# Four dense units, index items, stream loads and key turns moved forward in two stages of a streaming encoder

## What is computed

```python
s = einsum('bqhd,bld->bqhl', qi, ki) * (IDX_DIM ** -0.5)      # 8 index heads of 64
score = einsum('bqhl,bqh->bql', relu(s), w)                   # masked by chunks of 64 frames
_, idx = lax.top_k(score, topk)                               # 256 of up to 1024; streams: 132 of 528
logits = einsum('bqhgd,bqjhd->bqhgj', q, k_sel) * (A_HEAD_DIM ** -0.5)
p = softmax(where(valid, logits, -inf))
o = einsum('bqhgj,bqjhd->bqhgd', p, v_sel)                    # 16 heads, 4 key/value heads, of 64
```

## Time and profile before

| | us |
|---|---|
| median of 3 runs | 3180.77 (3178.53 to 3181.86) |
| the profiled execution | 3184.14 |
| its span, first to last instruction | 3182.3 |
| proj0b, SP's first issue to its last round's end | 104.2 to 347.7 |
| attention, first issue to last output | 349.0 to 759.9 |

### The profile page before, as it was taken

How to read it: one execution, slowest core, us unless ns; L and a number is a source line. 1 busy time by engine, 2 the same in 40 slices (tenths; PEclk the granted TensorE clock), 3 DMA queues, 4 the chain that set the end, 5 groups by cost and what they waited for, 6 DMA issues and landing times. The chain is left out here.

```text
span 3182.3 us, 45684 instructions
## 1 busy us (share of the span) xinstructions
PE 2982.0 (94%) x17935; PEld 2769.5 (87%) x17935; DVE 1612.6 (51%) x2629; ACT 927.6 (29%) x1640; POOL 699.6 (22%) x404
## 2 busy tenths in 40 slices
PE   8799489997999999999998999988899999999999
PEld 8699478887989999899997989987799999899897
DVE  3499689994253444444434145544334443444435
ACT  3332255664132112121123044433132112121122
POOL 2111010110212111121112145545222111211112
PEclk9899799998999999999999999998999999999999
DMA  4421521123211110111102233327321110110101
GB/s 139 97 73 56 139 60 28 33 49 134 77 63 40 40 53 26 53 40 40 53 27 105 69 111 103 100 84 273 122 68 49 39 53 26 53 48 31 53 28 72
DMA packets 196202, 222.96 MB, mean 70 GB/s; under 512 B 27793, under 2 KB 172113, under 8 KB 196066
## 3 DMA queue, kind: packets, MB, share of 16 engines
q1 hardware_dynamic: 155666, 157.13, 16.1%
q10 hardware_dynamic: 40400, 63.97, 6.1%
HBM read 171.11 MB, written 49.95 MB: 69 GB/s over the span
## 5 line engine op out<-in xcount | busy, mean ns | idle before, releaser
L769 DVE TENSOR_TENSOR h<-mlp_dn_acc,h 128x512 f32<-128x512 f32 x576 | 397.5, 691 | 339.5 <-PE mlp_dn_acc L739 339.5
L758 DVE TENSOR_TENSOR mlp_sq<-mlp_relu 128x384 f32<-128x384 f32 x192 | 165.9, 864 | 555.8 <-ACT mlp_relu L662 555.8
L724 PE MATMUL mlp_up_acc<-mid_xT_hi,mid_w_hi 128*128 128x384 f32 x768 | 258.0, 336 | 2.3 <-PEq L69 2.3
L724 PE MATMUL mlp_up_acc<-end_xT_hi,end_w_hi 128*128 128x384 f32 x768 | 257.9, 336 | 2.3 <-PEq L69 2.3
L662 ACT ACTIVATE mlp_relu<-mlp_up_acc 128x384 f32<-128x384 f32 x192 | 94.5, 492 | 563.1 <-PE mlp_up_acc L724 563.1
L724 PE MATMUL mlp_up_acc<-mid_xT_hi,mid_w_lo 128*128 128x384 f32 x768 | 257.8, 336 | 0.0
L724 PE MATMUL mlp_up_acc<-mid_xT_lo,mid_w_hi 128*128 128x384 f32 x768 | 257.8, 336 | 0.0
L724 PE MATMUL mlp_up_acc<-end_xT_hi,end_w_lo 128*128 128x384 f32 x768 | 257.7, 335 | 0.0
L724 PE MATMUL mlp_up_acc<-end_xT_lo,end_w_hi 128*128 128x384 f32 x768 | 257.6, 335 | 0.0
L739 PE MATMUL mlp_dn_acc<-mid_w_hi,mlp_hid_hi 128*128 128x512 f32 x576 | 224.7, 390 | 0.0
L739 PE MATMUL mlp_dn_acc<-mid_w_lo,mlp_hid_hi 128*128 128x512 f32 x576 | 224.5, 390 | 0.0
(11 more groups left out here) (277 smaller groups left out, 7380.6 us busy)
## 6 DMA issues: line engine op xcount, KB each, us to landing
mid_w_raw<-in_ffn_w_up ACTq DMA_DIRECT2D x15, 1024.0 KB, 5.3
mid_w_raw<-in_ffn_w_down ACTq DMA_DIRECT2D x15, 1024.0 KB, 5.0
end_w_raw<-in_ffn_w_up ACTq DMA_DIRECT2D x15, 1024.0 KB, 5.3
end_w_raw<-in_ffn_w_down ACTq DMA_DIRECT2D x15, 1024.0 KB, 4.9
mid_w_raw<-in_b_w_in SPq DMA_DIRECT2D x11, 1024.0 KB, 7.0
proj_w_raw<-in_a_w_in SPq DMA_DIRECT2D x8, 1024.0 KB, 6.3
att_q_in<-qT SPq DMA_DIRECT2D x16, 512.0 KB, 7.9
qT<-proj0b_stage SPq DMA_DIRECT2D x24, 192.0 KB, 1.8
```

Of the source, the lines that this page charges most:

```text
L724: mm = pe.matmul(up_acc[:, u % 3, 0:GW], w_up_s[a][:, k, j * P:(j + 1) * P], x_s[c][:, k, g * GW:(g + 1) * GW], start=(n == 0), stop=(n == ...
L758: dve.tensor_tensor(sq[:, u % 2, :], relu[:, u % 2, :], relu[:, u % 2, :], ALU.mult)\
L769: dve.tensor_tensor(cols, dn_acc[:, v % 3, :], cols, ALU.add).then_inc(added, 1)
```

## The change

- Planner of proj0b: `FIRST = 4` units are taken out of the plan and stand ahead of everything else on TensorE, ScalarE (copies) and SP (stores). `LEAD` goes from 1.0 to -3.0, and VectorE's costs are multiplied by `SLOWER = 1.14`.
- SP in attention: streams 3, 4, 5 are loaded between the two query loads and the values, 6 and 7 right behind.
- Attention on TensorE: `turn_prompt_keys` ahead of `logits(n)`. On VectorE: `prompt_keys_lo` ahead of the mask of item n.

```diff
-LEAD = 1.0
+LEAD = -3.0
...
-        plan, units = [], list(gm.units)
+        FIRST = 4
+        plan, units = [], list(gm.units[FIRST:])
...
+        SLOWER = 1.14
...
-                pe_time, dve_time = pe_time + 0.11 * (t + 1), dve_time + 0.15 * (t + 1) + 0.1
+                pe_time, dve_time = pe_time + 0.11 * (t + 1), dve_time + SLOWER * (0.15 * (t + 1) + 0.1)
                 while dve_time < pe_time + LEAD:
                     took = a_round(NUMBER[t])
                     if not took:
                         break
-                    dve_time += took
+                    dve_time += SLOWER * took
...
                 took = a_round(len(CHOICE))
                 if not took:
                     break
-                dve_time += took
+                dve_time += SLOWER * took
...
                 gm.sp_load_w(sp, 1)
+                for u in gm.units[:FIRST]:
+                    gm.sp_store(sp, u)
...
-                        if t is gm.of[t["c"]][0]:
+                        if t is gm.of[t["c"]][0] or t["i"] == FIRST:
                             gm.sp_load_w(sp, t["c"] + 2)
...
             def _(pe):
+                for u in gm.units[:FIRST]:
+                    gm.pe_unit(pe, u)
                 pe.wait_ge(ki_loaded, 32)
...
+                for u in gm.units[:FIRST]:
+                    gm.act_evacuate(act, u)
                 for r in range(2):
                     act.wait_ge(turned, r + 1)
...
                 load_stream(2)
+                load_stream(3)
                 load_q(0)
+                load_stream(4)
+                load_q(1)
+                load_stream(5)
                 sp.dma_start(vin[:, :, :], v_out.rearrange("(t p) c -> p t c", p=P)).then_inc(v_loaded, 16)
-                load_q(1)
-                for s in range(SR, DEC_B):
-                    load_stream(s)
+                load_stream(6)
+                load_stream(7)
...
+                    if n in PREP:
+                        turn_prompt_keys(PREP[n])
                     if 0 <= n < N:
                         logits(n)
-                    if n in PREP:
-                        turn_prompt_keys(PREP[n])
...
                         t, L = tile_at(n), length(n)
+                        if n in PREP:
+                            prompt_keys_lo(PREP[n])
                         dve.wait_ge(qk_done, n + 1)
...
-                        if n in PREP:
-                            prompt_keys_lo(PREP[n])
                         for tt in rounds_at[n]:
                             ch.dve_round(dve, tt)
```

## The result

The kernel after takes 3223.3 us (median of 4 runs, 3220.0 to 3226.3), the kernel before 3181.3 on the same chip (3178.5 to 3183.1): ratio 1.013, 95% interval 1.0117 to 1.0143. It is slower by 42 us where +34.3 was forecast. The profiled execution took 3223.32 us, with a span of 3221.5; that of the kernel before took 3184.14, 2.8 above its median, so the two spans differ by 39.2 us only.

A forecast was written before the change was run, and what follows sets the result against it. Proj0b was taken to end on VectorE, with attention's fuller tiles near full on both VectorE and TensorE. Terms -18.2 (proj0b), -17 (sample tile) and +69.5 (lumps) gave +34.3 on 3180.8: 3215.1 us, range 3196 to 3236.

The forecast's parts named there:

- lumps are carried over: Rival, attention: TensorE and ScalarE work on through lumps, so only VectorE's total counts (+21 us); 3167 us, chance 0.05.
- half hidden: Rival, attention: only 35 of the 69.5 us lost to lumps remain; 3181 us, no change, chance 0.06.
- the loads merely change places: Rival, sample tile: stream keys wait for query loads, gain 3 instead of 17; 3229 us, 0.22 together with the other smaller-gain rival.
- proj0b gains little: Rival, proj0b: dense index items bind VectorE or small loads come later, gain about 3; 3230 us, 0.22 together with loads rival.
- Proj0b, -18.2 forecast: Proj0b: TensorE ends the phase, VectorE 10 us ahead; attention starts at 330.8 instead of 349.0 us; bounds 12 to 23.
- the charge for dense index items: Proj0b: 2 us added to TensorE's remaining 202.4 us, for index items waiting on VectorE.
- The first index item: Proj0b: start at 122.4 us, 6.1 later than before, after four units, key turns and the copy chain.
- the 1.5 us for a start at half clock: Proj0b start: 1.5 us added to the four units' 11.5 us for a slow first unit; bounds 0 and 11.5.
- The sample tile, -17 forecast: Attention's first tile: the 8.5 us cached-key wait and 9.8 us of prompt-key waits go; 17 us gained, bounds 8 and 22.
- the 1.3 us for later loads being late: Sample tile: 1.3 us charged because later stream loads, interleaved with large loads, may each be a little late.
- The lumps, +69.5 forecast: Attention: rounds bunched in tiles 5 (+16.2), 1 (+27.7) and 0 (+29.8), less savings elsewhere; 69.5 us lost, bounds 45 and 75.
- the clock term (+2): Attention: tiles 4, 3 and 2, entered after a lump, lose 2 us together, range 0 to 6.

The follow-up runs named there:

- The same work lumped: The kernel before, with the 19 rounds lying in tile 3 moved into tile 0, three an item from its end: 3199.16 us, ratio 1.0052.
- evenly dealt kernel: The kernel after, with attention's 152 rounds dealt evenly within each tile and tiles 4, 1, 3, 0 given 16, 16, 13, 19: 3184.46 us, ratio 0.9999.

## Why the prediction was right, and where it was off

**The sign and its cause.** Right. 16 rounds left proj0b, and `rounds_at` made lumps in tiles 5, 1 and 0; VectorE works in order and TensorE can't run ahead. The total was closer than its parts deserve: as said below, two of them were met partly by luck. After the lump of tile 0 TensorE stands idle for 3.39 us ahead of the first matmul of tile 2, waiting for a mask, as the earlier trace rows showed for three rounds in one item:

```profile
777.16 0.69 PE L1433 MATMUL att_slot<-att_k_hi,att_q_split 128*128 128x384 f32 x1 [3.39 <-DVE att_neg_max L1594]
```

The same work lumped costs 15.5 us, and dealt evenly it gives some 40 back. That rejects the two rivals in which lumps are carried over or half hidden. That the loads merely change places is rejected by the kernel with the loads alone (5.8 us gained in tile S, no wait for cached keys over 2.8 inside it); that proj0b gains little holds in part, as follows.

**Proj0b, -18.2 forecast, -13.5 measured.** Which engine ends the phase was right, if by 2.7 us only, and so were the 4.0 us from TensorE's end to the next phase. The step that failed is the charge for dense index items, 2 us: TensorE needed 209.5 us for the 202.4 left, so 7.1. Of these, 3.2 are additional idle time; the rest I can't place (the clock is 0.98 in both kernels). The kernel with `LEAD` alone shows the same at full size (12.2 us idle). And in the kernel with four units ahead alone TensorE needed 322.4 - 123.1 = 199.3 us, less than the 202.4, with index items and units mixed.

VectorE's end shows the same mistake. The prediction took 37.0 us of rounds off its 218.2 and had it end at 316.7; it ended at 328.8, though its wait for the small loads was over 2.7 us earlier than forecast (132.8 for 135.5). It needed 196.0 us and not 181.2, and 13.1 of these 14.8 us are additional idle time. So both engines waited for each other through the relu copies. The prediction counted the dense items as a bound from VectorE's total; it should have read the three relu buffers and two banks as it read the two items and four buffers of attention.

The first index item, 122.0 for 122.4, is partly luck. The first unit began at 105.19 and not at 103.9, and the 1.5 us for a start at half clock didn't occur in this execution; the two cancel. In the profiles of the seven other kernels with four units ahead it did occur: the four took 13.2 to 14.2 us there and 11.7 here (see the last section). It wouldn't have mattered for the end: in the evenly dealt kernel, whose proj0b is the same program, the first index item came at 124.66, and TensorE ended at 331.7 for 331.5.

**The sample tile, -17 forecast, -17.4 measured: right in size by luck, not in its parts.** With the old plan both edits give 12.8 us, 4 fewer than forecast. Inside the tile the waits for cached keys then fall from 9.1 to 5.3 us, by 3.8 where 8.5 - 1.3 = 7.2 were forecast: the 1.3 us for later loads being late were too few. Those for the prompt keys fall from 9.8 to 2.7, not to nothing. With the new plan they fall to 0.5, and those for cached keys to 4.3. The edits then give 10.4 us (81.6 to 71.2), and the remaining 7 of the 17.4 come with the new plan, which the prediction had at nothing. It also read the 12.5 us of the earlier trace rows as the tile's own, though 3.5 of them end ahead of its first mask; and its sign "no wait over 3 us for cached keys" was missed, with 4.3 us ahead of the tile and 3.1 in it.

**The lumps, +69.5 forecast, +71.6 measured.** Tiles 1 and 0 are within 2 us, tile 4 within 0.2. Tile 5 is 2.7 longer, tile 3 falls 3.1 further, to TensorE's own time. What the prediction called the clock term (+2) is within these. That placement and amount are separate, about 42 and 30 us, it did not say; the even dealing showed it.

**The factor 1.14.** That rounds don't suffer from GpSimd holds: in the kernel after a MAX8 of 1024 elements takes 1.23 us beside a GpSimd subtraction and 1.22 just behind one (the rows are in the last section). The Trainium skill (GPSIMD Engine Reference, 8 Key points) has GpSimd contend with VectorE instructions in a two-port mode or with two SBUF inputs; MAX8 reads one tensor, and the trace agrees. The prediction let the planner move the rounds all the same and gave that no price of its own; in time, the factor costs 29 us net.

## What to carry to other kernels

When a planner leaves work for a second planner, follow its output through both: a small shift in the first can become lumps in the second. A running slack that lets work pile up for later assumes that the other engines can run ahead by as much, so compare it with the buffers between them; where they allow only two items, deal the work evenly over the items. And a stage whose engines are interleaved through two or three buffers loses time when one kind of item is put densely in front, even if no engine's total is above the stage's length.

## What was unexpected of the hardware

- How fast TensorE starts after a short idle time differs between executions. The first unit of the kernel after ran at full clock (1.00, 3.1 us) after TensorE had been idle for 3.52 us. In the seven other kernels with four units ahead it ran at 0.50 to 0.68 and took 4.2 to 5.5 us, after the same 3.5 us, and two of those have the same proj0b. One of these two is the evenly dealt kernel:

```profile
105.38:110.84 5.46, 5.46 (x25) 5.46 (x26) 0.00 (x0) 0.00 (x0) 0.00 (x0) 0.50 0.73 165
```

  The first unit of the other phase, after 3.15 us, ran at a mean of 0.64. So the length of the idle time alone doesn't tell here how a stretch starts, and one profile doesn't either.
- An index item's addition that starts while GpSimd subtracts isn't just slower; it ends shortly after GpSimd does. Its instructions and GpSimd's in the kernel after (start, us), where four of the same form took 4.38 us in a row (1.1 each):

```profile
165.23 4.38 DVE L1182 SCALAR_TENSOR_TENSOR score<-proj0b_relu,proj0b_w,score 128x768 f32<-128x768 f32 x4
...
173.01 2.92 DVE L1182 SCALAR_TENSOR_TENSOR score<-proj0b_relu,proj0b_w,score 128x768 f32<-128x768 f32 x1 [3.40 <-ACT proj0b_relu L1122]
175.86 1.22 DVE L814 MAX8 proj0b_top<-score 128x8 f32<-128x1024 f32 x1
...
260.59 1.23 DVE L814 MAX8 proj0b_top<-score 128x8 f32<-128x1024 f32 x1
...
259.02 4.61 POOL L360 TENSOR_TENSOR proj_w_lo<-proj_w_raw,proj_w_hi 128x2048 fp32r<-128x2048 f32 x1 [20.38 <-ACT proj_w_hi L353]
...
170.58 4.54 POOL L360 TENSOR_TENSOR proj_w_lo<-proj_w_raw,proj_w_hi 128x2048 fp32r<-128x2048 f32 x1 [6.25 <-ACT proj_w_hi L353]
...
125.42 5.00 POOL L360 TENSOR_TENSOR proj_w_lo<-proj_w_raw,proj_w_hi 128x2048 fp32r<-128x2048 f32 x1
```

  GpSimd's subtraction ends at 175.12 and VectorE's addition at 175.93. The same holds for all ten additions that start inside such a subtraction, six before (one is in the earlier trace rows) and four after: they take 2.6 to 4.2 us and end 0.3 to 1.1 us behind it. The first index item of the kernel after, at 125.22, starts 0.2 us ahead of the subtraction of 125.42 and takes its 0.75 us. So what an addition loses depends on how much of the subtraction is left when it starts, and one that starts first loses nothing. VectorE's index work fell from 58.7 to 51.0 us in proj0b, with four such additions for six.
- In the lumped tiles the granted clock is 0.66 and 0.61, in tile 0 of the even kernel still 0.68 at three quarters TensorE busy. Between the two levels (1.2 and 2.4 GHz, so 0.5 and 1.0) such a mean says that it changed within the tile. VectorE is busy 93%, 87% and 96% of these three tiles, so there is little time in them that this lost clock could have cost.
- With 16 rounds dealt evenly tile 4 was shorter than with 7 in a bunch (36.5 us for 38.4), with 35.7 us of VectorE work under 35.0 of TensorE. The clock may be the reason: it was 0.95 there for 0.91, which my estimate from these two puts at some 1.6 us. It wasn't tested apart.
